# Eight row buffers with VectorE's PSUM copies in the load stage, and three value heads of the delta rule convolved by TensorE

## The reference

```python
h = rmsnorm(x, g_mix)                       # x: (1, 1024, 1024)
dq, dk, dv, dz, db, da, ... = split(h @ w_in)
qkv = silu(causal_depthwise_conv(concat([dq, dk, dv]), conv_w))   # 4 taps, each of 3*512 channels by itself
q = l2norm(dq.reshape(b, s, 4, 128)) * 128 ** -0.5
k = l2norm(dk.reshape(b, s, 4, 128))
v = dv.reshape(b, s, 4, 128)
beta = sigmoid(db)
g = -exp(a_log) * softplus(da + dt_bias)
o_dn = gated_delta_rule_chunked(q, k, v, beta, g)
```

## Time and profile before

| | us |
|---|---|
| median of 3 runs (3604.36 to 3606.14) | 3605.76 |
| the profiled execution | 3607.95 |
| its span in the profile | 3606.2 |
| TensorE busy (93% of the span) | 3341.4 |
| VectorE busy (50%) | 1791.2 |
| ScalarE busy (34%) | 1219.4 |
| GpSimd busy (30%) | 1071.6 |

### The profile page before, as it was taken

The page is one execution under the profiler, slowest core; times in us unless marked ns, Lnnn a source line. Parts: engine busy times, 40 slices in busy tenths (PEclk is TensorE's granted clock), DMA queues, the critical chain, the costliest instruction groups (busy, mean ns, idle before and its releaser), DMA issues. The chain is left out here.

```text
span 3606.2 us, 46994 instructions
## 1 busy us (share of the span) xinstructions
PE 3341.4 (93%) x18342; PEld 2649.7 (73%) x18342; DVE 1791.2 (50%) x3378; ACT 1219.4 (34%) x2265; POOL 1071.6 (30%) x589
## 2 busy tenths in 40 slices
PE   7799898799989899999999989999898999998988
PEld 5478676699878787888888867776666677775667
DVE  1788788654554426554554580234454402345443
ACT  3465566544222312000000040334453212344540
POOL 3133000154445335453543433220112333201112
PEclk9899999699899999999999999999999999999999
DMA  3111100000312114232221213110102211101011
GB/s 118 30 36 35 32 6 1 8 1 2 104 47 71 36 35 148 65 99 70 81 93 58 64 36 100 47 41 13 24 1 76 82 44 57 53 13 18 8 71 70
DMA packets 234300, 179.90 MB, mean 50 GB/s; under 512 B 42944, under 2 KB 219248, under 8 KB 233216
## 3 DMA queue, kind: packets, MB, share of 16 engines
q1 hardware_dynamic: 231376, 176.56, 15.9%
q10 hardware_dynamic: 2736, 0.78, 0.1%
HBM read 159.92 MB, written 16.87 MB: 49 GB/s over the span
## 5 line engine op out<-in xcount | busy, mean ns | idle before, releaser
L1102 DVE SCALAR_TENSOR_TENSOR y_T<-y_T 128x1024 f32<-128x1024 f32 x48 | 137.4, 2915 | 0.1
L881 ACT ACTIVATE I-13450a_hi<-I-13449act_f 128x512 fp32r<-128x512 f32 x22 | 13.5, 634 | 338.5 <-DVE I-13449act_f L890 338.5
L914 DVE TENSOR_TENSOR x_T<-x_T,I-13456p_d 128x512 f32<-128x512 f32 x88 | 60.4, 688 | 126.2 <-PE I-13456p_d L846 126.2
L283 PE MATMUL I-13454p_g<-hf_hi,I-13430w_hi 128*128 128x512 f32 x352 | 108.8, 390 | 3.4 <-POOL hf_lo L523 3.4
L283 PE MATMUL I-13455p_u<-hf_hi,I-13431w_hi 128*128 128x512 f32 x352 | 108.9, 391 | 2.3 <-POOL I-13433w_lo L269 2.3
L285 PE MATMUL I-13455p_u<-hf_lo,I-13431w_hi 128*128 128x512 f32 x352 | 109.2, 392 | 0.0
L287 PE MATMUL I-13455p_u<-hf_hi,I-13433w_lo 128*128 128x512 f32 x352 | 108.8, 390 | 0.0
L285 PE MATMUL I-13454p_g<-hf_lo,I-13430w_hi 128*128 128x512 f32 x352 | 108.4, 389 | 0.0
L287 PE MATMUL I-13454p_g<-hf_hi,I-13432w_lo 128*128 128x512 f32 x352 | 108.4, 389 | 0.0
L890 DVE TENSOR_TENSOR I-13449act_f<-I-13448act_g,I-13455p_u 128x512 f32<-128x512 f32 x44 | 28.3, 684 | 156.6 <-PE I-13455p_u L287 156.6
L1697 DVE TENSOR_TENSOR I-22508S<-I-22508S,c_causal 128x256 f32<-128x256 f32 x32 | 13.8, 431 | 185.0 <-PE I-22508S L1622 185.0
(11 more groups left out here) (1390 smaller groups left out, 10175.1 us busy)
## 6 DMA issues: line engine op xcount, KB each, us to landing
y_T<-in_w_ada SPq DMA_DIRECT2D x48, 512.0 KB, 3.6
saved_x<-x_T SPq DMA_DIRECT2D x3, 4096.0 KB, 13.6
I-13428w_raw<-in_w_gate SPq DMA_DIRECT2D x22, 512.0 KB, 4.6
I-13429w_raw<-in_w_up SPq DMA_DIRECT2D x22, 512.0 KB, 4.1
x_T<-saved_x SPq DMA_DIRECT2D x2, 4096.0 KB, 14.1
I-13442d_raw<-in_w_down SPq DMA_DIRECT2D x11, 512.0 KB, 4.8
I-13443d_raw<-in_w_down SPq DMA_DIRECT2D x11, 512.0 KB, 4.8
I-895w_raw<-in_w_in SPq DMA_DIRECT2D x8, 512.0 KB, 3.8
```

Of the source, the lines that this page charges most:

```text
L283: nc.tensor.matmul(out[h], w_hi[:, k, :], hi(k, h), start=(k == 0), stop=False)
L881: nc.scalar.activation(a_hi[s][:, cols], act_f[:, cols], ACT.Copy).then_inc(a_rounded, 1)
L914: nc.vector.tensor_tensor(x_n, x_n, p_d[n % 2][:, h, :], ALU.add).then_inc(d_added[n % 2], 1)
L1102: self.nc.vector.scalar_tensor_tensor(out=self.raw[s], in0=self.raw[s], scalar=1.0, in1=self.c_row, op0=ALU.mult, op1=ALU.mult, accum_out= ...
```

## The change

In the load stage each of the eight tiles gets a buffer, SyncE issues the eight reads one behind the other with no wait, and the loops of SyncE and TensorE are written out. ScalarE keeps the squares alone; VectorE, which had nothing there, copies the turned tiles out of PSUM.

In the delta inputs' stage:

- V of heads 0 to 2 is convolved by TensorE. GpSimd multiplies the identity by each tap's column, twelve diagonal matrices of 128x128 (`diagonals`). A head is then eight f32 matmuls, four taps for each half of 512 tokens, summed in PSUM; they use the two tiles of the later spreads (`ir.wide`). ScalarE takes the Silu straight from PSUM (`silu_of_pe`), two of three among the other convolutions. V of head 3 stays with VectorE, so that `order` has nine entries, all before the root.
- The sums of squares change form: the squares are the moving operand, 512 columns at a time, and the stationary operand is `pick`, eight columns with ones in column g. All eight groups add up in one PSUM tile `p_totals`, [8, 1024]. At the end ScalarE copies it to `totals`, and TensorE turns it in eight transposes to the layout that the root needs. There are three `sq` tiles instead of two.
- Ln moves from the start of ScalarE's stream behind the last Silu. The four copies of the sparse attention's result stand behind the root.

The diff, cut to its core:

```diff
 def load_stage(nc, const, src, tiles, dst, small, row_sums):
-        rows = [st.sb(f"rows{s}", [P, D]) for s in range(2)]
+        rows = [st.sb(f"rows{t}", [P, D]) for t in range(tiles)]
...
-                for i in peeled(sp, tiles // 2):
-                    for s in range(2):
-                        wait(sp, turned[s], i)
-                        wait(sp, squared[s], i)
-                        sp.dma_start(rows[s][:, :], src[ds((2 * i + s) * P, P), :]).then_inc(row_in[s], 16)
+                for t in range(tiles):
+                    sp.dma_start(rows[t][:, :], src[t * P:(t + 1) * P, :]).then_inc(row_in[t], 16)
...
+                for t in range(tiles):
+                    pe.wait_ge(row_in[t], 16)
+                    wait(pe, copied, t - 1)
+                    for k in range(KD):
+                        last = nc.tensor.transpose(tps[t % 2][:, k, :], rows[t][:, k * P:(k + 1) * P], const["c_ident"][:, :])
+                    last.then_inc(turned, 1)
...
+                for t in range(tiles):
+                    act.wait_ge(row_in[t], 16)
+                    wait(act, squared, t - 1)
+                    nc.scalar.activation(unread[t % 2][:, :], rows[t][:, :], ACT.Square, accum_out=row_sums[:, t:t + 1]).then_inc(squared, 1)
+            @block.vector
+            def _(dve):
+                for t in range(tiles):
+                    dve.wait_ge(turned, t + 1)
+                    nc.vector.tensor_copy(dst[:, :, t * P:(t + 1) * P], tps[t % 2][:, :, :]).then_inc(copied, 1)

 def delta_inputs_stage(...):
+    ON_PE = DN_HEADS - 1
-    order = [(b, h) for h in range(DN_HEADS) for b in (Q, K)] + [(V, h) for h in range(DN_HEADS)]
+    order = [(b, h) for h in range(DN_HEADS) for b in (Q, K)] + [(V, ON_PE)]
...
+            @block.gpsimd
+            def _(pool):
+                for h in range(ON_PE):
+                    for back in range(CONV_K):
+                        nc.gpsimd.tensor_tensor(diagonals[:, h, back, :], const["c_ident"][:, :], tap(V, h, back).to_broadcast([P, P]), ALU.mult).then_inc(diagonal_set, 1)
+                    if h == 0:
+                        (pick: a memset to 0, a wait for it, a memset of its diagonal to 1)
+
             @block.tensor
             def _(pe):
+                def convolve(h, part):
+                    out, first = ir.wide[h % 2], part * BANK
+                    if part == 0:
+                        pe.wait_ge(diagonal_set, CONV_K * (h + 1))
+                        wait(pe, v_done, h - 1)
+                    for back in range(CONV_K):
+                        at = max(first, back)
+                        last = nc.tensor.matmul(out[:, at:first + BANK], diagonals[:, h, back, :], raw[V][:, h, at - back:first + BANK - back],
+                                                start=(back == 0), stop=(back == CONV_K - 1))
+                    if part == HALVES - 1:
+                        last.then_inc(pe_convolved, 1)
+
+                def row_sum(g):
+                    if g == 0:
+                        pe.wait_ge(pick_set, 2)
                     pe.wait_ge(squared, g + 1)
-                    ir.pe_sum(pe, g, sq[g % 2])
+                    for part in range(HALVES):
+                        last = nc.tensor.matmul(p_totals[0:N, part, :], pick[:, g, :], sq[g % 3][:, part * BANK:(part + 1) * BANK], start=(g == 0), stop=(g == N - 1))
+                    last.then_inc(row_summed, 1)
+
+                (order: convolve 0,0 0,1; sum 0; convolve 1,0; sum 1; convolve 1,1; sums 2, 3;
+                 convolve 2,0; sums 4, 5; convolve 2,1; sums 6, 7)
+                pe.wait_ge(totals_out, 1)
+                for t in range(NT):
+                    last = nc.tensor.transpose(ir.sums[:, t * N:(t + 1) * N], totals[:, t * P:(t + 1) * P], const["c_ident"][0:N, 0:N])
+                last.then_inc(ir.summed, 1)
+                pe.wait_ge(v_done, ON_PE)
                 for g in range(N):
                     ir.pe_spread(pe, g)
...
+                def silu_of_pe(h):
+                    act.wait_ge(pe_convolved, h + 1)
+                    nc.scalar.activation(v_T[:, h, :], ir.wide[h % 2], ACT.Silu).then_inc(v_done, 1)
...
-                own(nc.scalar.activation(t1[:, :, :], t1[:, :, :], ACT.Ln, bias=const["c_ones"][:, 0:1]))
                 own(nc.scalar.activation(a_log[:, :], a_log[:, :], ACT.Exp))
...
-                        wait(act, ir.summed, g - 1)
-                        nc.scalar.activation(sq[g % 2][:, :], x, ACT.Square).then_inc(squared, 1)
-                    if n == N:
-                        ir.act_root(act)
+                        wait(act, row_summed, g - 2)
+                        nc.scalar.activation(sq[g % 3][:, :], x, ACT.Square).then_inc(squared, 1)
+                    if n in (3, 5):
+                        silu_of_pe((n - 3) // 2)
+                silu_of_pe(2)
+                own(nc.scalar.activation(t1[:, :, :], t1[:, :, :], ACT.Ln, bias=const["c_ones"][:, 0:1]))
+                act.wait_ge(row_summed, N)
+                nc.scalar.activation(totals[:, :], p_totals[0:N, :, :].rearrange("p h n -> p (h n)"), ACT.Copy).then_inc(totals_out, 1)
+                ir.act_root(act)
                 for h in range(DN_HEADS):
                     nc.scalar.activation(sparse_y[:, h, :], sparse_T[:, h, :], ACT.Copy)
...
-                for n in range(N + 2):
+                for n in range(len(order)):
                     convolve(n)
...
-                ir.dve_invert(dve)
+                dve.wait_ge(ir.summed, 1)
+                (the variance from ir.sums, with the order of its columns changed)
+                ir.dve_refine(dve)
                 for g in range(N):
                     scaled(g)
-                    if g % 4 == 1:
-                        convolve(N + 2 + g // 4)
```

More of the change, by code:

```diff
@@ L313, in load_stage @@
     with stage(nc) as st:
-        rows = [st.sb(f"rows{s}", [P, D]) for s in range(2)]
+        rows = [st.sb(f"rows{t}", [P, D]) for t in range(tiles)]
         tps = [st.ps(f"tps{s}", [P, KD, P]) for s in range(2)]
         unread = [st.sb(f"squares{s}", [P, D]) for s in range(2)]
-        squared = st.two("squared")
-        small_in, ident_in = st.sem("small_in"), st.sem("ident_in")
-        row_in, turned, copied = st.two("row_in"), st.two("turned"), st.two("copied")
+        small_in, ident_in, row_in = st.sem("small_in"), st.sem("ident_in"), [st.sem(f"row_in{t}") for t in range(tiles)]
+        squared, turned, copied = st.sem("squared"), st.sem("turned"), st.sem("copied")
         with nc.Block() as block:
@@ L322, in _ @@
             def _(sp):
-                if small:
-                    sp.dma_start(*small[0]).then_inc(ident_in, 16)
-                for i in peeled(sp, tiles // 2):
-                    for s in range(2):
-                        wait(sp, turned[s], i)
-                        wait(sp, squared[s], i)
-                        sp.dma_start(rows[s][:, :], src[ds((2 * i + s) * P, P), :]).then_inc(row_in[s], 16)
-                if small:
-                    sp.wait_ge(small_in, 16 * len(small[1:]))
+                sp.dma_start(*small[0]).then_inc(ident_in, 16)
+                for t in range(tiles):
+                    sp.dma_start(rows[t][:, :], src[t * P:(t + 1) * P, :]).then_inc(row_in[t], 16)
+                sp.wait_ge(small_in, 16 * len(small[1:]))
             @block.tensor
             def _(pe):
-                if small:
-                    pe.wait_ge(ident_in, 16)
-                for i in peeled(pe, tiles // 2):
-                    for s in range(2):
-                        pe.wait_ge(row_in[s], 16 * (i + 1))
-                        wait(pe, copied[s], i)
-                        for k in range(KD):
-                            last = nc.tensor.transpose(tps[s][:, k, :], rows[s][:, k * P:(k + 1) * P], const["c_ident"][:, :])
-                        last.then_inc(turned[s], 1)
+                pe.wait_ge(ident_in, 16)
+                for t in range(tiles):
[4 more added lines that the diff above has]
+                    last.then_inc(turned, 1)
             @block.scalar
@@ L348, in _ @@
                     act.dma_start(tile, at).then_inc(small_in, 16)
-                for i in range(tiles // 2):
-                    for s in range(2):
-                        act.wait_ge(row_in[s], 16 * (i + 1))
-                        wait(act, squared[s], i)
-                        nc.scalar.activation(unread[s][:, :], rows[s][:, :], ACT.Square, accum_out=row_sums[:, 2 * i + s:2 * i + s + 1]).then_inc(squared[s], 1)
-                        act.wait_ge(turned[s], i + 1)
-                        nc.scalar.activation(dst[:, :, ds((2 * i + s) * P, P)], tps[s][:, :, :], ACT.Copy).then_inc(copied[s], 1)
+                for t in range(tiles):
[7 more added lines that the diff above has]
+                    nc.vector.tensor_copy(dst[:, :, t * P:(t + 1) * P], tps[t % 2][:, :, :]).then_inc(copied, 1)
 def keep_running(nc, n, out, stationary, moving):
@@ L2779, in _ @@
             @block.tensor
```

(19 more changed lines are left out.)

17 lines of the change are left out of this document (15 added, 2 removed).

## The result

The kernel after takes 3580.57 us (median of 4 runs, 3577.95 to 3583.28) against 3605.95 before (4 runs, 3604.36 to 3606.21): a ratio of 0.9929, 95% interval 0.9918 to 0.9941, some 25 us faster. The profiled execution took 3583.08, against the 3594.0 that the sum gave for it.

The account below looks back on a forecast made before the run. It took the load stage as bound by reads waiting for two buffers, the delta inputs' stage by VectorE's convolutions and ScalarE's late copies. Gains 10.5 + 3.5 = 14.0 us took the median 3605.76 to 3591.8; range 3582 to 3598.

Parts of the forecast that it names:

- bound by reads waiting for two buffers: Load stage before: reads that wait for one of two buffers set its time, not an engine; forecast gain 10.5 us.
- squares would hide: Load stage: ScalarE's eight squares end at 17.4 us, hidden behind TensorE's transposes.
- I take the low clock: Load stage: TensorE's transposes stay at the low clock, 1.73 us a tile, for a gain of 10.5 us.
- the bound that I had set aside (13.0): Load stage: if the clock rises, the data set the end at 18.6 us and the gain is about 13.0.
- I take 3.6: Delta inputs' stage: nine GpSimd operations each hold up one VectorE tap by 0.40, 3.6 us; bounds 0 and 3.6.
- Its own sign of being wrong: Delta inputs' stage: some nine taps of about 1.68 us instead of 1.28; wrong if taps stay at 1.28.
- TensorE's last sum (39.6): Delta inputs' stage: TensorE ends its sums at 663.2, just after VectorE's last convolution (661.8); ScalarE's Ln ends at 665.5.
- Transposes of the totals: Delta inputs' stage, before the root: eight transposes of 8 rows, between 1.1 and 1.9 us, taken as 1.5.
- the steps from the variance to the first spread: Delta inputs' stage, the root: 2.2 us from the variance to the first spread, which starts at 670.2.
- the third spread: End of the delta inputs' stage: spreads start cold as before, the third 5.94 us after the first.
- All that follows ... only moves earlier: Everything behind either changed stage stands behind a barrier and only moves earlier.
- rival (1): Charges too high: no VectorE hold-up (3.6), clock open through the gap (2.4), load follows data (2.5); 3583 to 3589; chance 0.22.

Follow-up runs that it names:

- e5: Kernel after, but in the load stage ScalarE copies the tiles as before, eight buffers kept; 3587.38 us (one execution).
- e6: Kernel before, but in the load stage VectorE copies out of PSUM, two buffers kept; 3604.15 us (one execution).
- e7: Kernel after, with GpSimd making each diagonal of the second and third head once more into a spare buffer; 3579.13 us (one execution).
- e8: Kernel after, with eight more GpSimd operations of 128x512 behind the diagonals, into a spare buffer; 3592.45 us (one execution).
- e1: Kernel before with the new load stage alone; 3596.28 us, ratio 0.9964.
- e2: Kernel before with the new delta inputs' stage alone; 3595.55 us, ratio 0.9967.
- e12: Kernel before, unchanged, profiled once more; 3610.61 us.
- e3: Kernel after, unchanged, run and profiled again; 3579.53 us, ratio 0.9923.

## Why the prediction was wrong

**Load stage, 2.6 of the miss.** That it was bound by reads waiting for two buffers, and that squares would hide, is shown by e5 and e6. The step that failed is "I take the low clock". The clock rose at the fourth tile of dense transposes, and the bound that I had set aside (13.0) came in at 13.1. That eight transposes took as long in the last tile as in the first goes with the gaps between tiles, as I had noted and then not used: in e6, with those gaps, the last three tiles take 1.97 again. The Trainium skill ("TensorE: Matmul & The Clock Gate", "Part 4: PE-mode transpose") says that transposes don't open the clock; here TensorE did nothing but transposes up to then (each one record in the trace, where an f32 matmul is two), and the time of eight went from 1.91 to 1.06. The trace disagrees with the rule.

**Delta inputs' stage, 3.9.** The failed step is "I take 3.6": nine taps held up by a whole GpSimd operation each. The ninth convolution ended 35.0 after the first tap, not 38.2; the charge was some 0.4. Its own sign of being wrong came: three taps took 4.09 at most, 1.36 each and not 1.68. The row behind it was of operations some six times as long, and e7, e8 and the stage of that row show that what VectorE loses is the length less 0.2 to 0.3, which leaves almost nothing of 0.4. The mechanism was right and its size was not: one ratio from long operations doesn't carry to short ones. Of these 3.2 us 0.4 were lost again. By the prediction's sum TensorE's last sum (39.6) came 2.3 ahead of ScalarE's Ln; it came at 38.9, 0.3 behind it, so TensorE ended last of the two, by 0.4 at the copy. Transposes of the totals were 0.7, not 1.5; the steps from the variance to the first spread 2.5, not 2.2; the third spread came 5.28 after the first, not 5.94. The spreads did start cold (3.60 for the first).

**What came as forecast.** TensorE's 512-column matmuls warmed the clock in the stage (0.92 over it; half a convolution, four matmuls, takes 3.70), the copy on VectorE 1.23, the last square's end 17.5, the order of gains and their independence (e1, e2). Of the 16.2 at which the last read was to land, 16.0 was measured.

**"All that follows ... only moves earlier", 4.4.** This holds for its start and not for its length. The untouched 3.5 ms changed by -4.4 us in the profiled pair, and the leftovers of the timed kernels run from -2.3 to +6.7. e12 and e3 show changes of that size between executions of one program. Whether the new delta inputs' stage itself makes some of it is open, and would be worth a run of its own: the last stretch took 1485.0 to 1488.6 in the five profiles with the old delta inputs' stage, and 1478.1 to 1484.8 in seven of the eight with the new one (1486.4 in e8), and the medians of the whole change leave 5 and 7 us above the stages' gain. No run shows a cause for that.

Of the cases on record it was rival (1), at two of its three places, together with a gain behind the stages that no case had. Rival (1) adds up wrongly: two of its places give at most 6.1 us, 3585.7; its 3583 takes all three. The two stages' misses alone, 2.6 and 3.9, would have brought 3585.3, inside the range; it was the untouched part, 4.4 in the profiled pair and perhaps chance, that carried the time below 3582. Nothing had been set aside for it.

## What to carry to other kernels

Count a GpSimd operation beside a VectorE one of two SBUF inputs by its own length when alone, less 0.2 to 0.3 us (four lengths from 0.37 to 2.39 here), not by a share taken from longer ones; small ones are nearly free, wide ones are not. When a charge upstream falls away, look at every queue that had only just been hidden, not at the one that the bracket names: here two ended 0.3 us apart, and moving work out of both was worth 3.9 us of the stage. And for a gain of under 1% in a program of milliseconds, read the stage: the same program's untouched part moved by up to 7 us.

## What was not expected of the hardware

- Transposes alone bring TensorE to the high clock when they are dense: 1.91 us for eight, then 1.34, then 1.06, from about 11 us on. In e6, with waits between tiles, one tile came to 1.17 and the next fell back to 1.97; in e5 the last four stayed at 1.06 to 1.07, with waits of 0.9 between them.
- GpSimd and VectorE take turns: 1.31 to 1.37 us for a GpSimd operation that needs 0.37 alone, while the VectorE tap beside it loses 0.06; it loses 0.70 of 1.04, 1.70 of 1.90 and 2.20 of 2.39 beside longer ones.
- Eight reads of 512 KB issued some 0.5 us apart, with none waiting for another, land with the last at 16.0, and TensorE starts on the last three 1.34 to 1.36 us apart.
- A matmul of 512 columns with a stationary of only 8 columns takes what one of 128 takes (1.88 for two matmuls, against 3.70 for four of the convolution).
